# Second residual gate folded into the projection's weights, with three last weight chunks held together

## The chip, the cores and the metric

The kernel runs on one core of one Trainium2 chip. The metric is the device time of one execution in microseconds (us). The engines are named as in the profile: PE is TensorE (PEld its weight loads), DVE is VectorE, ACT is ScalarE, POOL is GpSimd, SP is SyncE, which issues nearly all DMAs.

## The reference, cut to what matters

Two model blocks follow each other on 512 tokens of width 1024, all in float32. The change is in the second layer of the first block, latent attention, and in what comes directly behind it:

```python
# mla_mixer: 16 heads of 128 values
o = jnp.einsum('bshr,rhd->bshd', o_lat, w_uv).reshape(B, S, MLA_WIDTH)   # 512 x 2048
return (o * jax.nn.silu(z)) @ w_out                                       # w_out is 2048 x 1024

# first_block, layer l = 1
x = layer_norm(DEEPNORM_ALPHA * x + (1.0 + gate[:, None, :]) * y, ln_g[l], ln_b[l])

# second_block begins
bcx = rmsnorm(h, a_pre_norm[l]) @ w_in        # b_gate, c_gate, u = split(bcx)
```

The gate is one row of 1024 values, the same for all tokens, so multiplying column n of y by 1 + gate[n] equals multiplying column n of w_out by it.

## The kernel before, in words

**Products in three parts.** A float32 product is made of three matmuls in a 32-bit fast format (`mm3`, lines 1818 to 1822): each operand is split in a high part (the value rounded) and a low part (the rest). A left operand tile is 128x128, a right one 128x512.

**The weight ring.** All weights pass through a ring of two slots, in chunks of 128x2048 values (1 MB). For each chunk SP loads `w_raw` (two DMAs, line 421) as soon as the semaphore `raw_free` of the slot says that the old chunk is split. ACT writes the high part `w_high` (`split_high`, line 743) when the load has landed (`w_full`) and PE has finished the slot's old chunk (`used`). POOL writes the low part `w_low` in eight slices of 128x256 (`low`, line 639), then frees `w_raw`. PE waits for `w_split`. At a few places DVE does the low part in one instruction (`split_low`, line 1183). Each engine's program is written out in a fixed order and only semaphores tie them together.

**The last pass of attention.** The loop over pairs of heads ends with pass `attend(7)`. It makes eight softmax units u = 0 to 7: PE scores, DVE takes the maximum (`top`), ACT exponentiates (`weigh`), DVE divides (`norm`), PE turns the result (line 2199), ACT copies it back, PE weighs values (line 2168). Between them PE does pieces of the gate projection z. In this pass ACT makes `w_high` of the projection's first chunk at u = 3.

**The projection `oout`.** Its weights are eight chunks, c = 0 to 7; chunk c holds the rows of heads 2c and 2c+1 and lies in slot c % 2. The left operand is `o_high`/`o_low`: for heads 2 to 15, ACT (line 959) and DVE (line 1529, `low_o`) make them one head at a time at the start of the projection. PE sums into eight PSUM banks, two for each tile of 128 tokens. A part, one chunk on one token tile, is 12 matmuls, and a chunk on all four tiles is 48. `out_stage` does chunks 0 to 5 on all tiles. It holds the last two chunks, 6 and 7, together: both on tile 0 and tile 1 first (tile 0's sum is then complete), and then on tiles 2 and 3:

```python
for t in range(2): part(0, t)                       # chunk 6
for t in range(2): part(1, t).then_inc(y_ready, 1)  # chunk 7: tiles 0 and 1 are complete
part(0, 2); part(0, 3); part(1, 2); part(1, 3)      # each with its increment
turn(0); turn(1)                                    # only in "oout"
```

**The boundary behind it.** For each token tile DVE multiplies the sum by the gate into `hf` (`ln_gated`, line 1426) and adds it to the scaled x (`ln_stats`, line 1431). ACT squares and takes the root (`ln_root`), DVE normalises (`ln_affine`, lines 1448 and 1449), ACT squares again (`square_x`), DVE writes `x_hat` (`prenorm`, line 1461), PE turns it (line 1949), ACT and DVE make `h_high` and `h_low` (`high_tile` line 896, `low_tile` line 1453). PE then does the first weights of the next projection, `cu`, on token tiles 0 and 1 (its two chunks, 96 matmuls of 256 columns), turns tile 2 after the first of them and tile 3 after the second, and waits for tile 3's `h_low` before it does the same two chunks on tiles 2 and 3 (the second halves). DVE makes half of the low part of `cu`'s second chunk (`split_half`, line 1389), POOL the other half (line 677).

## Time and profile before

| | before |
|---|---|
| median of three runs | 1877.47 us (1877.35 to 1878.3) |
| the profiled execution | 1876.41 us, of which the span is 1874.3 us |
| PE busy | 1807.3 us, 96% of the span |
| PEld, DVE, ACT, POOL busy | 80%, 42%, 40%, 42% |
| attention's last pass, then the projection | PE at 635.7 to 663.3 us, then to 751.4 us |
| boundary | the second halves of `cu` begin at 777.1 us |

Spans are told from the first instruction. The idle time of an engine stands in brackets behind the instruction that ended it, with what released it. Idle time of an engine that is not the bottleneck costs nothing.

### The profile page before, as it was taken

The page shows a single profiled execution, that of the slowest core. Times are in us where ns is not written, and L with a number is a line of the kernel's source. Part 1 is how long each engine was busy: PE and PEld are TensorE (multiplying, and loading weights), DVE is VectorE, ACT ScalarE, POOL GpSimd, SP SyncE. Part 2 cuts the span into 40 slices and gives each one's busy share as a digit, 9 for nine tenths or more (in the row PEclk, how much of TensorE's full clock was granted, in tenths as well). Part 3 has the DMA queues.
Part 4 walks back from the last instruction along what each step waited for, and adds up shares of the span by engine and source line. Part 5 has one row for each costly group of instructions (what it writes and reads, how often), then busy time and mean ns, then how long its engine had stood idle before and what let it go on. Part 6 is the DMA issues. An engine that isn't in the chain of part 4 may idle for free.

```text
span 1874.3 us, 24002 instructions
## 1 busy us (share of the span) xinstructions
PE 1807.3 (96%) x8798; PEld 1494.8 (80%) x8798; DVE 791.5 (42%) x1388; ACT 746.1 (40%) x1043; POOL 788.9 (42%) x992
## 2 busy tenths in 40 slices
PE   6999999989999999899999999999997999999998
PEld 6788878878788878788888888888965788888886
DVE  5775775367677632623241111103678341111102
ACT  3423331365656542322253344214456453443212
POOL 0375454354101162355335555443443135555351
PEclk9999999999999999999999999999999999999999
DMA  9543565221212132233233343232311133433321
GB/s 314 172 135 90 151 202 183 93 82 37 73 36 73 45 124 90 68 93 132 90 91 90 93 109 112 102 112 82 114 45 45 46 91 90 109 92 90 120 94 67
DMA packets 209320, 190.94 MB, mean 102 GB/s; under 512 B 10475, under 2 KB 189538, under 8 KB 209250
## 3 DMA queue, kind: packets, MB, share of 16 engines
q1 hardware_dynamic: 208608, 189.69, 32.7%
q8 instruction: 46, 0.75, 0.2%
q10 hardware_dynamic: 642, 0.29, 0.1%
q14 instruction: 24, 0.20, 0.0%
HBM read 187.86 MB, written 2.10 MB: 101 GB/s over the span
## 4 chain that ended last, share of the span: by engine, by line
PE 86%; DVE 5%; ACT 3%; POOL 3%; issue 2%; DMA 0%; SPq 0%; ACTq 0%; POOLq 0%; DVEq 0%
PE PS L1820 27%; PE PS L1822 26%; PE PS L1821 26%; POOL w_low L639 2%; PE PS L2168 1%; ACT w_high L743 1%; PE PS L1949 1%; PE PS L2199 1%; POOL w_low L677 1%; DMA ada_raw<-in_ada_w 0%; DVE soft L1775 0%; DVE probs L1773 0%; PE PS L2359 0%; PE PS L2191 0%; PE PS L2190 0%
## 5 line engine op out<-in xcount | busy, mean ns | idle before, releaser
L639 POOL TENSOR_TENSOR w_low<-w_raw,w_high 128x256 fp32r<-128x256 f32 x905 | 701.6, 811 | 841.2 <-ACT w_high L743 841.2
L1820 PE MATMUL PS<-h_high,w_high 128*128 128x512 f32 (+1 forms) x1488 | 560.7, 377 | 15.4 <-DVE h_low L1453 7.0
L1821 PE MATMUL PS<-h_low,w_high 128*128 128x512 f32 (+1 forms) x1488 | 553.7, 372 | 0.0
L1822 PE MATMUL PS<-h_high,w_low 128*128 128x512 f32 (+1 forms) x1488 | 553.6, 372 | 0.0
L743 ACT ACTIVATE w_high<-w_raw 128x2048 fp32r<-128x2048 f32 (+2 forms) x150 | 280.2, 1868 | 683.8 <-PE PS L1822 669.1
L1820 PEld LDWEIGHTS PS<-h_high,w_high 128*128 128x128 f32 x1488 | 281.6, 189 | 68.6 <-DVE h_low L1453 8.3
L1822 PEld LDWEIGHTS PS<-h_high,w_low 128*128 128x128 f32 x1488 | 281.5, 189 | 48.8
L1821 PEld LDWEIGHTS PS<-h_low,w_high 128*128 128x128 f32 x1488 | 281.8, 189 | 45.7 <-issue 0.7
L1363 DVE TENSOR_TENSOR gate_buf<-gate_buf,PS 128x512 f32<-128x512 f32 x44 | 30.3, 688 | 334.9 <-ACT gate_buf L876 334.3
L1183 DVE TENSOR_TENSOR w_low<-w_raw,w_high 128x2048 fp32r<-128x2048 f32 (+1 forms) x15 | 33.3, 2220 | 325.4 <-ACT w_high L743 325.4
L1820 PE MATMUL PS<-w_high,ff_high 128*128 128x512 f32 x352 | 137.2, 390 | 0.1
L1822 PE MATMUL PS<-w_high,ff_low 128*128 128x512 f32 x352 | 137.0, 389 | 0.0
L1821 PE MATMUL PS<-w_low,ff_high 128*128 128x512 f32 x352 | 137.0, 389 | 0.0
L667 POOL TENSOR_TENSOR w_low<-w_raw,w_high 128x256 fp32r<-128x256 f32 x35 | 29.8, 882 | 165.0 <-ACT w_high L743 165.0
L1820 PEld LDWEIGHTS PS<-w_high,ff_high 128*128 128x128 f32 x352 | 66.1, 188 | 14.6 <-POOL w_low L639 1.0
L1821 PEld LDWEIGHTS PS<-w_low,ff_high 128*128 128x128 f32 x352 | 66.1, 188 | 13.7
L1822 PEld LDWEIGHTS PS<-w_high,ff_low 128*128 128x128 f32 x352 | 66.1, 188 | 13.6
L1820 PE MATMUL PS<-w_high,o_high 128*128 128x512 f32 x192 | 75.5, 393 | 0.6 <-POOL w_low L639 0.6
L1821 PE MATMUL PS<-w_low,o_high 128*128 128x512 f32 x192 | 74.8, 389 | 0.0
L1822 PE MATMUL PS<-w_high,o_low 128*128 128x512 f32 x192 | 74.8, 389 | 0.0
L977 ACT ACTIVATE probs<-PS,soft 128x128 f32<-128x128 f32 (+1 forms) x64 | 33.8, 528 | 75.8 <-DVE soft L1573 75.8
L1367 DVE TENSOR_TENSOR ff_low<-gate_buf,ff_high 128x512 f32 x44 | 41.9, 953 | 40.8 <-ACT ff_high L880 40.8
(310 smaller groups left out, 2574.8 us busy)
## 6 DMA issues: line engine op xcount, KB each, us to landing
w_raw<-in_f_gate_up SPq DMA_DIRECT2D x88, 512.0 KB, 4.9
w_raw<-in_f_down SPq DMA_DIRECT2D x40, 512.0 KB, 4.3
w_raw<-in_e_w_in SPq DMA_DIRECT2D x32, 512.0 KB, 5.0
gains<-in_ada_w SPq DMA_DIRECT2D x16, 1024.0 KB, 5.2
w_raw<-in_a_w_in SPq DMA_DIRECT2D x24, 512.0 KB, 4.5
w_raw<-in_o_w_in SPq DMA_DIRECT2D x20, 512.0 KB, 4.3
ada_raw<-in_ada_w SPq DMA_DIRECT2D x8, 1024.0 KB, 13.3
w_raw<-in_e_w_out SPq DMA_DIRECT2D x16, 512.0 KB, 5.6
```

The source lines that it names most:

```text
L639: ins = nc.gpsimd.tensor_tensor(WL[s][:, piece], raw[s][:, piece], WH[s][:, piece].bitcast(F32), ALU.subtract)
L667: ins = nc.gpsimd.tensor_tensor(WL[1][:, piece], raw[1][:, piece], WH[1][:, piece].bitcast(F32), ALU.subtract)
L677: nc.gpsimd.tensor_tensor(WL[1][:, h:], raw[1][:, h:], WH[1][:, h:].bitcast(F32), ALU.subtract).then_inc(pool_half, 1)
L743: nact(WH[s][:, 0:n], raw[s][:, 0:n], ACT.Copy).then_inc(w_high[s], 1)
L977: nact(pm[u % 2][:, 0:w], PS[:, 2 + u % 2, 0:w], ACT.Exp, scale=MLA_SCALE, bias=soft[:, u % 2, 1, 0:1], accum_out=soft[:, u % 2, 2, 0:1]). ...
L1183: v.tensor_tensor(WL[s][:, 0:size], raw[s][:, 0:size], WH[s][:, 0:size].bitcast(F32), ALU.subtract).then_inc(w_split[s], 1)
L1363: v.tensor_tensor(buf[s][:, :], buf[s][:, :], PS[:, 2 * s + 1, :], ALU.mult).then_inc(prod_ready, 1)
L1367: v.tensor_tensor(lows[:, f, :], buf[s][:, :], fH[:, f, :].bitcast(F32), ALU.subtract).then_inc(gate_low, 1)
L1820: mm(dst, lh, rh, start=first, stop=False, skip_group_check=True)
L1821: mm(dst, lh, rl, start=False, stop=False, skip_group_check=True)
L1822: return mm(dst, ll, rh, start=False, stop=last, skip_group_check=True)
L1949: ins = tr(two(2 * t if b is None else b)[:, k, :], src[:, k * P:(k + 1) * P], ident)
```

## The change

- DVE multiplies the raw weights of each projection chunk by the gate row, in place (`gate_weights`), a 128x2048 instruction for each of the eight chunks; ACT makes `w_high` only then (new semaphores `w_gated`). The first two stand in the last pass of attention, between `top` and `norm` of u = 3 and of u = 6. The third and fourth stand between the `low_o` of heads 5 and 6 and of heads 9 and 10. The last four stand behind all heads.
- At the boundary `ln_gated` and `ln_stats` become one instruction reading PSUM (`ln_join`).
- Chunks 5, 6 and 7 are held together. Chunk 5's high and low parts go to two new tiles (`spareH`, `spareL`). PE does all three on tiles 0 and 1 first, then the five remaining parts but one, the turns of tiles 0 and 1, and the last part (chunk 7 on tile 3) behind these turns.
- ACT makes `w_high` of chunk 0 at u = 4 instead of u = 3, and of chunk 7 before chunk 6. DVE now makes the low part of chunk 6 as well as of chunk 7.
- `cu` leaves the list of projections whose second chunk is shared: POOL makes all of its low part, in eight slices, and DVE's half goes.

```diff
-        SHARED = ["cu", "gu0", "kv", "gu1"]
+        SHARED = ["gu0", "kv", "gu1"]
...
                 if name == "oout":
-                    first = 1
-                    low(0, 0)
-                    low(0, 1)
+                    for c in range(5):
+                        low(c // 2, c % 2)
+                    pool.wait_ge(w_high[1], B.split[1] + 3)
+                    for c in range(0, CHUNK, SLICE):
+                        piece = slice(c, c + SLICE)
+                        ins = nc.gpsimd.tensor_tensor(spareL[:, piece], raw[1][:, piece], spareH[:, piece].bitcast(F32), ALU.subtract)
+                    ins.then_inc(w_split[1], 1)
+                    pool.wait_ge(w_split[1], B.split[1] + 3)
+                    pool.sem_inc(raw_free[1], 1)
+                    continue
...
-                act.wait_ge(w_full[s], B.full[s] + (i + 1) * (16 * B.dmas[s]))
+                if name == "oout" and i < B.pairs:
+                    act.wait_ge(w_gated[s], i + 1)
+                else:
+                    act.wait_ge(w_full[s], B.full[s] + (i + 1) * (16 * B.dmas[s]))
...
-            highs_of("oout")
+            for c in (2, 3, 4):
+                split_high("oout", c // 2, c % 2)
+            act.wait_ge(w_gated[1], 3)
+            nact(spareH[:, :], raw[1][:, :], ACT.Copy).then_inc(w_high[1], 1)
+            act.wait_ge(w_gated[1], 4)
+            act.wait_ge(used[1], B.use[1] + 2)
+            nact(WH[1][:, :], raw[1][:, :], ACT.Copy).then_inc(w_high[1], 1)
+            split_high("oout", 3, 0)
...
+            def gate_weights(c):
+                s, B = c % 2, BASE["oout"]
+                dve.wait_ge(w_full[s], B.full[s] + (c // 2 + 1) * (16 * B.dmas[s]))
+                dve.wait_ge(gate_ready, 2)
+                w = raw[s][:, :].rearrange("p (k n) -> p k n", n=D)
+                v.tensor_tensor(w, w, gate_bc[1].unsqueeze(1).broadcast_to((P, 2, D)), ALU.mult).then_inc(w_gated[s], 1)
...
+                    if u in (3, 6) and not more:
+                        gate_weights(u // 6)
...
             for h in range(2, HEADS):
                 low_o(h)
+                if h in (5, 9):
+                    gate_weights(2 + h // 9)
+            for c in (4, 5, 7):
+                if c == 7:
+                    gate_weights(6)
+                gate_weights(c)
             split_last("oout")
+            split_low("oout", 3, 0)
             n, q = T, TR["oout"]
-            ln_gated(1, "oout", 0)
-            ln_stats(0)
-            ln_gated(1, "oout", 1)
-            ln_stats(1)
+            ln_join(0)
+            ln_join(1)
             ln_affine(n + 1, 0)
             ln_affine(n + 2, 1)
             prenorm(n + 3, 0, 3, q, x_hat1)
-            ln_gated(1, "oout", 2)
             prenorm(n + 4, 1, 3, q, x_hat1)
             low_tile(q, 0, 0)
-            ln_stats(2)
+            ln_join(2)
             low_tile(q, 1, 2)
-            ln_gated(1, "oout", 3)
-            split_half("cu")
             ln_affine(n + 5, 2)
-            ln_stats(3)
+            ln_join(3)
...
+            for c in range(5):
+                heads_ready(c)
+                for t in (2, 1, 0, 3):
+                    if c == 0:
+                        attended(t)
+                    ins = head_part(c, t)
+                ins.then_inc(used[c % 2], 1)
+            for c in (5, 6, 7):
+                heads_ready(c)
+                for t in range(2):
+                    ins = head_part(c, t)
+                    if c == 7:
+                        ins.then_inc(y_ready, 1)
+            head_part(6, 2)
+            head_part(6, 3).then_inc(used[0], 1)
+            head_part(5, 2)
+            head_part(7, 2).then_inc(y_ready, 1)
+            head_part(5, 3).then_inc(used[1], 1)
+            turn(0)
+            turn(1)
+            head_part(7, 3).then_inc(used[1], 1)
```

## Rows read from the trace of the kernel before

**Rows 1.** The profile's page: the chain that ended last, by engine.
```profile
PE 86%; DVE 5%; ACT 3%; POOL 3%; issue 2%; DMA 0%; SPq 0%; ACTq 0%; POOLq 0%; DVEq 0%
```

**Rows 2.** PE in order of time: start, duration, then operation; last pass, projection's start.
```profile
659.70 0.63 PE L2199 MATMUL PS<-small,probs 128*128 128x128 f32 x4 [0.62 <-DVE probs L1579]
...
663.26 0.47 PE L1820 MATMUL PS<-w_high,o_high 128*128 128x512 f32 x1
...
674.02 0.39 PE L1822 MATMUL PS<-w_high,o_low 128*128 128x512 f32 x1
675.03 0.50 PE L1820 MATMUL PS<-w_high,o_high 128*128 128x512 f32 x1 [0.62 <-POOL w_low L639]
```

**Rows 3.** Busy time by stretch (PE, PEld, DVE, ACT, POOL, granted clock, DMA share, GB/s).
```profile
675.00:751.00 76.00, 75.97 (x335) 62.90 (x336) 20.20 (x25) 20.66 (x21) 30.90 (x42) 1.00 0.31 97
```

**Rows 4.** PE in order of time at the boundary.
```profile
751.38 1.04 PE L1949 MATMUL PS<-small,x_hat 128*128 128x128 f32 x8
753.34 1.09 PE L1949 MATMUL PS<-small,x_hat 128*128 128x128 f32 x8 [0.92 <-DVE x_hat L1461]
757.71 0.38 PE L1820 MATMUL PS<-h_high,w_high 128*128 128x256 f32 x1 [3.28 <-DVE h_low L1453]
...
767.05 1.09 PE L1949 MATMUL PS<-small,x_hat 128*128 128x128 f32 x8 [1.86 <-DVE x_hat L1461]
...
773.73 1.03 PE L1949 MATMUL PS<-small,x_hat 128*128 128x128 f32 x8
777.14 0.39 PE L1820 MATMUL PS<-h_high,w_high 128*128 128x256 f32 x1 [2.37 <-DVE h_low L1453]
```

**Rows 5.** Busy time by stretch, columns as in rows 3: behind PE's idle time.
```profile
757.00:763.00 6.00, 5.29 (x31) 5.29 (x32) 5.89 (x6) 1.71 (x4) 2.98 (x2) 0.72 0.67 182
```

**Rows 6.** DVE instructions by line: shortest, median and longest in ns, first and last start.
```profile
L1183 DVE TENSOR_TENSOR w_low<-w_raw,w_high x15: 2018/2292/2293, 16.0 to 1847.2; 128x2048 fp32r<-128x2048 f32 x11, 128x1792 fp32r<-128x1792 f32 x4
L1529 DVE TENSOR_TENSOR o_low<-o_gated,o_high x16: 678/1213/1227, 661.5 to 679.0; 128x512 fp32r<-128x512 f32 x16
```

**Rows 7.** DVE in order of time in attention's last pass.
```profile
648.41 0.15 DVE L1573 TENSOR_SCALAR soft<-soft 128x1 f32<-128x1 f32 x1
649.41 0.16 DVE L1578 RECIPROCAL soft<-soft 128x1 f32<-128x1 f32 x1 [0.85 <-ACT probs L977]
649.61 0.49 DVE L1579 TENSOR_SCALAR probs<-probs,soft 128x512 f32<-128x512 f32 x1
...
656.63 0.11 DVE L1571 MEMSET PS<- 64x64 f32 x1
...
658.70 0.86 DVE L1579 TENSOR_SCALAR probs<-probs,soft 128x512 f32<-128x512 f32 x1
```

**Rows 8.** SP, then ACT, in order of time: the third chunk's load.
```profile
665.69 0.33 SPq L549 DMA_DIRECT2D gains<-in_ln_g  x1
...
675.28 1.92 ACT L743 ACTIVATE w_high<-w_raw 128x2048 fp32r<-128x2048 f32 x1 [1.84 <-DMA w_raw<-in_o_w_out]
```

**Rows 9.** POOL in order of time: the second, third and fourth chunk's low parts.
```profile
666.22 8.76 POOL L639 TENSOR_TENSOR w_low<-w_raw,w_high 128x256 fp32r<-128x256 f32 x8 [5.40 <-ACT w_high L743]
677.28 7.02 POOL L639 TENSOR_TENSOR w_low<-w_raw,w_high 128x256 fp32r<-128x256 f32 x8 [2.30 <-ACT w_high L743]
...
699.22 5.59 POOL L639 TENSOR_TENSOR w_low<-w_raw,w_high 128x256 fp32r<-128x256 f32 x8 [5.29 <-ACT w_high L743]
```

**Rows 10.** The shared halves by line, DVE then POOL: shortest, median, longest ns.
```profile
L1389 DVE TENSOR_TENSOR w_low<-w_raw,w_high x4: 1224/1226/2432, 758.8 to 1506.2; 128x1024 fp32r<-128x1024 f32 x4
L677 POOL TENSOR_TENSOR w_low<-w_raw,w_high x4: 2386/3444/3447, 757.8 to 1506.2; 128x1024 fp32r<-128x1024 f32 x4
```

**Rows 11.** A later load's issue on SP, then two stretches (columns as in rows 3).
```profile
684.53 0.86 SPq L421 DMA_DIRECT2D w_raw<-in_o_w_out  x2
...
688.50:689.50 1.00, 1.00 (x7) 0.81 (x6) 0.00 (x0) 0.00 (x0) 1.00 (x2) 1.00 0.43 176
689.50:691.50 2.00, 2.00 (x10) 1.68 (x9) 0.00 (x0) 0.00 (x0) 2.00 (x4) 1.00 0.00 0
```

**Rows 12.** DVE and ACT in order of time at the boundary.
```profile
751.58 1.70 DVE L1461 SCALAR_TENSOR_TENSOR x_hat<-x,stat,gains 128x1024 f32<-128x1024 f32 x1
...
755.38 1.90 ACT L743 ACTIVATE w_high<-w_raw 128x2048 fp32r<-128x2048 f32 x1
...
765.39 1.13 ACT L908 ACTIVATE h_high<-x,mv 128x1024 fp32r<-128x1024 f32 x1
...
771.96 1.28 DVE L1461 SCALAR_TENSOR_TENSOR x_hat<-x,stat,gains 128x1024 f32<-128x1024 f32 x1
```

More of the change, by code:

```diff
@@ L298, in program @@
         oL = dz("o_low", 8192, [P, HEADS, S], F32R)
+        spareH, spareL = dz("w_high_spare", 16384, [P, CHUNK], F32R), dz("w_low_spare", 18432, [P, CHUNK], F32R)
         soft = dz("soft", 22400, [P, 2, 8, 4])
@@ L372, in program @@
             sem(n) for n in ("s_done", "m_ready", "e_ready", "p_ready", "t_done", "pT_ready", "pv_done", "sz_ready", "oz_ready"))
+        w_gated = [sem(f"w_gated{s}") for s in range(2)]
         z_dve, z_pool = sem("z_dve"), sem("z_pool")
@@ L994, in attend @@
                         nact(vh[:, :, :], PS[:, 6:8, :].rearrange("p a (b n) -> p (a b) n", b=2), ACT.Copy).then_inc(kv_ready, 1)
-                    if u == 3:
-                        split_high(*(("mla", i + 1) if more else ("oout", 0)), 0)
+                    if u == 3 and more:
+                        split_high("mla", i + 1, 0)
+                    if u == 4 and not more:
+                        split_high("oout", 0, 0)
                 act.wait_ge(used[1], B.use[1] + i + 1)
@@ L1016, in _ @@
                 high_o(h)
-            highs_of("oout")
+            B = BASE["oout"]
+            for c in (2, 3, 4):
[6 more added lines that the diff above has]
+            split_high("oout", 3, 0)
             load_sqrt()
@@ L1432, in ln_stats, with ln_join @@
                 v.tensor_scalar(mv[:, t, 0:1], mv[:, t, 1:2], 1.0 / D, None, ALU.mult).then_inc(ln_stat, 1)
+            def ln_join(t):
+                wait_y(dve, 1, "oout", t)
+                if t == 0:
+                    dve.wait_ge(x_ready, T)
+                xt = x[:, t, :]
+                steps.link(v.scalar_tensor_tensor(xt, xt, ALPHA, flat2(2 * t), ALU.mult, ALU.add, accum_out=mv[:, t, 1:2]))
+                v.tensor_scalar(mv[:, t, 0:1], mv[:, t, 1:2], 1.0 / D, None, ALU.mult).then_inc(ln_stat, 1)
             def ln_factor(n, t):
@@ L2248, in _, with heads_ready, head_part @@
             turn = turner("oout", 0, x_hat1)
-            out_stage("oout", oH, oL, lambda kt: pe.wait_ge(ol_ready, kt + 1), attended, turn=turn, order=(2, 1, 0, 3))
+            B = BASE["oout"]
+            def heads_ready(c):
+                pe.wait_ge(w_split[c % 2], B.split[c % 2] + c // 2 + 1)
+                pe.wait_ge(ol_ready, 2 * c + 2)
+            def head_part(c, t):
+                wh, wl = (spareH, spareL) if c == 5 else (WH[c % 2], WL[c % 2])
+                for d in range(2):
+                    for n in range(2):
+                        w = slice(d * D + n * S, d * D + (n + 1) * S)
+                        k, rows_ = 2 * c + d, slice(t * P, (t + 1) * P)
+                        ins = mm3(PS[:, 2 * t + n, :], oH[:, k, rows_], oL[:, k, rows_], wh[:, w], wl[:, w], k == 0, k == HEADS - 1)
+                return ins
+            for c in range(5):
[19 more added lines that the diff above has]
+            head_part(7, 3).then_inc(used[1], 1)
             in_stage("cu", (TR["oout"], turn))
```

## The prediction

> **What bounds the kernel now.** I read the chain that ended last first: 86% of it is PE, so time is lost or won only where PE stands idle or slow, and I look for such places around the change [rows 1]. In order of time, PE waits 0.62 us for softmax in the last pass of attention, and 0.62 us for a low part at the projection's second chunk [rows 2]. A chunk's 48 matmuls begin 0.229 us apart, or 10.9 us in all, from the first at 663.26 to the last at 674.02 [rows 2]. From there to 751 us PE is busy for 75.97 of 76.00 us [rows 3]: the projection is bound by its matmuls, and any weight chunk that comes late costs its whole delay. At the boundary PE waits four times, 0.92 + 3.28 + 1.86 + 2.37 = 8.43 us [rows 4], and behind the 3.28 us the granted clock falls: its mean is 0.72 over 6 us, so 0.28 x 6 = 1.7 us of full clock are missing [rows 5]. In that stretch PE then waits 1.86 us all the same, so these 1.7 us are hidden.
>
> **The boundary, which is the gain.** I count from the start of chunk 5, T0. Before, three chunks (12 parts of 12 matmuls, 2.72 us each) take 32.6 us up to 751.4 [rows 4], so T0 = 718.7 and the second halves of cu, at 777.14 [rows 4], stand at T0 + 58.4. After: tile 0 is complete at T0 + 13.6 and tile 1 at T0 + 16.3; five parts follow, and the turn of tile 0 is due at T0 + 29.9. The fused join saves a pass of DVE on each tile, and x_hat of tile 1 is ready at about T0 + 27.5, so the turns don't wait. The last part ends at 29.9 + 2 x 0.95 + 2.7 = T0 + 34.5. The join of tile 2 stands between the two low_tile on DVE, so h_low of tile 1 comes about 1.6 us later and the 3.28 shrink to 1.6. Tile 2 decides next. Its root stands behind cu's second w_high on ACT, which waits for the last part: 1.9 us [rows 12]. From the root's start to the end of x_hat one tile takes 765.39 to 773.24, 7.9 us [rows 12]. POOL now makes eight slices of cu meanwhile; a DVE instruction of this chain took 1.70 instead of 1.28 us beside such slices [rows 12], 0.4 each on two of them, 0.8. So tile 2 turns at T0 + 34.5 + 0.1 + 1.9 + 7.9 + 0.8 = T0 + 45.2. From there PE's own work and the last wait are as before: 773.73 - 767.05 = 6.7 and 777.14 - 773.73 = 3.4 us [rows 4]. Sum T0 + 55.3: a gain of 3.1 us. Its bounds: 1.5 us if the slices hold every two-input instruction, 4.5 us if neither they nor ACT's order cost anything.
>
> **The multiplies in softmax.** A multiply isn't in the trace. The nearest row is DVE's 128x2048 instruction with two inputs from SBUF, 2.29 us [rows 6]. The first begins at 648.56, when top(3) ends; norm(3) began at 649.41 and ended at 650.10 [rows 7]. It now ends at 648.56 + 2.29 + 0.7 = 651.55, 1.45 us later, and PE's turn of u = 3 and all behind it move with it. Of the second multiply about 1.1 us lie in DVE's wait for ACT. Top(7), at 656.63 before [rows 7], starts behind it at about 659.25: 2.6 us later, which nothing takes up (the 0.62 us of idle are of this chain). Moving chunk 0's w_high to u = 4 costs nothing, as it lies in ACT's wait before u = 7. So the projection begins 2.65 us later, at 665.9. Chunk 1's low part is then in time, because DVE stops after four heads to wait and POOL runs alone: the 0.62 us and some 0.2 us around it go. Chunk 1 starts **1.9 us late**, at 676.9, and PE wants chunk 2 at 687.9. Bounds of this term: 0 if the fillers take up the delay, 2.7 if chunk 1 still waits.
>
> **Chunk 2, the largest term.** SP sends the gains and then this chunk only behind the last gated head, from 665.69, and ACT got it at 675.28, having waited for the DMA [rows 8]: 9.6 us. Moved by 2.65 it lands at 677.9. Before, ACT made w_high at once and POOL ran from 677.28 to 684.3 [rows 9], 1.6 us ahead of PE. Now DVE multiplies first, to 680.2 (all behind it in DVE's queue, the heads 6 to 15, waits too), ACT takes 1.9 us and POOL begins at 682.2. Alone it needs 5.6 us [rows 9], which would be 687.8, just in time. It isn't alone: DVE has ten heads and the multiply of chunk 3 before it. That the two take turns, one instruction each, is in the rows: the eight slices beside low_o took 8.76 us [rows 9], so 1.15 us for each pair, and low_o took 1213 ns instead of 678 [rows 6]. And a long instruction holds the other for all its length: POOL's half takes 2386 ns alone and 3444 when DVE's of 1224 goes first; DVE's takes 2432 when POOL's goes first [rows 10]. So: 0.9 us to the end of the first slice, 2.15 for the multiply of chunk 3, 0.6 for a slice, and six pairs of 1.15 with the last six heads: 682.2 + 0.9 + 2.15 + 0.6 + 6.9 = 692.7. PE waits **4.8 us**. Bounds: 0 (POOL alone) and 6.5 (two slices more beside DVE, a landing 0.5 us later).
>
> The Trainium skill, "SBUF — State Buffer", section "SBUF: two separate sides", says that a DVE instruction with two SBUF inputs and a GpSimd instruction that reads SBUF hold a shared port pair by turns, each for the whole instruction, and don't share its bandwidth. [Rows 10] agree. By it the wait is the 4.8 us; read as a mere slowing of each POOL slice to 1.15 us, it would be 3.1.
>
> **The clock.** PE's idle 3.28 us at the boundary were followed by missing clock worth 1.7 us [rows 5]; I expect the same behind 4.8 us in the midst of full work: **+1.5 us**.
>
> **The last chunks.** A load takes 5.2 us from POOL's last slice to its end: POOL ends at 684.30, SP issues at 684.53, and the transfers are over at 689.5 [rows 9, 11]. From chunk 2's low part at 692.7: chunk 3 split at 698.3; chunk 5 landed 703.7, multiplied 706.0, its POOL part behind chunk 4's (712.8 with the slower clock) to 718.4; chunk 7 landed 723.8, multiplied 726.1, ACT makes chunk 7 and then chunk 6 to 730.0, DVE both low parts to 732.7. PE has done chunk 5 on tiles 0 and 1 at 732.3 and waits **0.5 us**. The wait falls on chunk 6, though it is chunk 7 that is late, as chunk 6 stands behind it on ACT. Bounds 0 and 3.
>
> **The sum.** 1.9 + 4.8 + 1.5 + 0.5 = 8.7 us lost, 3.1 won: 5.6 us slower. It passes to the end whole, as PE is the chain behind it. The profiled execution's 1876.4 (span 1874.3) become 1882.0; the runs' median lies 1.1 us above it: 1877.5 + 5.6 = **1883.1**.
>
> **The rivals.** (a) Chunk 2 is in time, because DVE and POOL hold each other less than I count. The wait and the clock's drop go, the tail costs 0.8: 1.9 + 0.8 - 3.1, so 1877.1, no difference. It decides whether chunk 2's low part ends before 687.9. Against it stand rows 10. (b) Faster: a multiply costs PE nothing, neither in softmax nor by holding POOL. The place is DVE's queue: its waits there, 0.85 us at a time [rows 7], would have to swallow a multiply, which is so only if it lasts under 0.9 us, against the 2.29 us of rows 6. Then there is no loss, the boundary gives 3.1 and its 0.8 us of slices: 1877.5 - 3.9 = 1873.6. For it speaks only that the trace holds no multiply of this form. (c) Slower still: the loads of chunks 5 and 7, in one chain now, come later than 5.2 us behind their release, towards the 9.6 us of the third chunk's [rows 8]; at 7.9 each it is 2 x 2.7 = 5.4 us more, 1888.5. Against it: no gains travel with them.
>
> **How the numbers follow.** The forecast has 0.62 (its own range 1880 to 1887), (a) 0.18, (b) 0.10, (c) 0.10. What a measurement of this kernel can tell from no change is 0.2%, 3.75 us. Faster by more: (b), 0.10. Within: (a) and 0.06 of the forecast, where the bounds of the boundary and chunk 2 meet, 0.24. Slower: 0.66. For 8 in 10 the range takes in (a) and leaves (b) and most of (c) out: 1876 to 1887.5.
>
> **What would show it.** In the profile after: norm of u = 3 ends about 1.5 us after it did, the projection begins near 665.9; PE's longest wait, near 5 us, stands at the third chunk and names POOL's w_low; POOL's slices there include one near 2.8 us; the granted clock falls behind it; PE waits under 3 us at chunk 6; the two turns don't wait; the waits at the boundary are near 1.6, 3 and 2.4 us. I am wrong if PE runs through chunk 2, or if the second halves come earlier than 777.1.

## The result and the profile after

The changed kernel takes 1882.34 us (median of 7 runs, 1880.90 to 1886.66), the kernel before 1876.77 us beside it (7 runs, 1875.12 to 1878.30). The ratio is 1.0032, with an interval of 1.0023 to 1.0042: it is slower, by 5.6 us between the medians and by 6.0 us by the ratio. The prediction was 5.6 us slower.

The profiled execution of the changed kernel took 1886.66 us, span 1884.9: the longest of its seven. Its steps are read one by one below; its sum is not the median's. 1.3 us of its excess arise before the change: POOL begins its last run of attention's weights at 630.69 in the trace of before and at 631.98 here. I count each trace from that run, R, and write an instant as R + so much.

The chain that ended last, by engine, of the kernel after:

```profile
PE 85%; DVE 5%; POOL 3%; ACT 3%; issue 1%; DMA 1%; SPq 0%; POOLq 0%; ACTq 0%; DVEq 0%
```

It is as in [rows 1]: PE still sets the end, so its waits are the account. PE's waits from 635 to 800 us of the kernel after, by what ended them: us in total, times, longest us.

```profile
PE PS L1862 <- POOL w_low L641: 3.8, 1, 3.8
PE PS L1862 <- DVE h_low L1484: 3.6, 2, 2.4
PE PS L1991 <- DVE x_hat L1492: 2.9, 1, 2.9
PE PS L2241 <- DVE probs L1617: 2.8, 2, 1.5
PE PS L2210 <- ACT probs_t L995: 0.8, 1, 0.8
PE PS L1862 <- DVE w_low L1205: 0.7, 1, 0.7
```

And PE in order of time, kernel after:

```profile
652.82 0.63 PE L2241 MATMUL PS<-small,probs 128*128 128x128 f32 x4 [1.23 <-DVE probs L1617]
...
663.21 0.63 PE L2241 MATMUL PS<-small,probs 128*128 128x128 f32 x4 [1.55 <-DVE probs L1617]
664.61 3.86 PE L2210 MATMUL PS<-probs_t,v_heads 128*128 128x512 f32 x8 [0.78 <-ACT probs_t L995]
...
668.23 0.48 PE L1862 MATMUL PS<-w_high,o_high 128*128 128x512 f32 x1
...
694.05 0.50 PE L1862 MATMUL PS<-w_high,o_high 128*128 128x512 f32 x1 [3.78 <-POOL w_low L641]
...
728.46 0.39 PE L1862 MATMUL PS<-w_high_spare,o_high 128*128 128x512 f32 x1
...
734.73 0.50 PE L1862 MATMUL PS<-w_high,o_high 128*128 128x512 f32 x1 [0.67 <-DVE w_low L1205]
...
765.23 0.39 PE L1862 MATMUL PS<-h_high,w_high 128*128 128x256 f32 x1 [1.22 <-DVE h_low L1484]
774.10 1.97 PE L1991 MATMUL PS<-small,x_hat 128*128 128x128 f32 x8 [2.86 <-DVE x_hat L1492]
...
786.93 0.51 PE L1862 MATMUL PS<-h_high,w_high 128*128 128x256 f32 x1 [2.37 <-DVE h_low L1484]
```

The projection begins at 668.23, R + 36.2, where [rows 2] have 663.26, R + 32.6: 3.7 us later. The 0.62 us at its second chunk [rows 2] are gone. The third chunk begins at 694.05 behind a wait of 3.78 us, the longest here; in [rows 3] there was none at all in this stretch. Chunk 6 costs 0.67 us. At the boundary one of the four waits of [rows 4] is gone, the 0.92 before tile 1's turn, and the 3.28 has become 1.22; but the wait for tile 2's x_hat has grown from 1.86 to 2.86, and the last is 2.37 as before. Chunk 5 begins at 728.46, R + 96.5, where T0 was 718.7, R + 88.0: 8.5 us later. The second halves of cu begin at R + 155.0, against R + 146.5 in [rows 4]: 8.5 us later too.

Part of this is the clock. Busy time by stretch (columns as in rows 3), kernel after:

```profile
664.00:668.00 4.00, 3.39 (x6) 1.82 (x7) 1.95 (x3) 3.97 (x6) 1.69 (x3) 0.57 0.00 0
694.00:700.00 6.00, 5.95 (x19) 4.73 (x20) 0.61 (x1) 0.00 (x0) 5.56 (x8) 0.72 0.52 175
773.00:780.00 7.00, 5.90 (x28) 5.90 (x29) 5.33 (x7) 3.28 (x7) 1.63 (x1) 0.53 0.54 150
786.00:792.00 6.00, 5.07 (x30) 5.07 (x30) 0.88 (x1) 0.00 (x0) 0.00 (x0) 0.72 0.01 3
```

The granted clock falls four times to its lower level: behind the short waits in softmax (0.43 x 4 = 1.7 us of full clock missing), behind the third chunk (0.28 x 6 = 1.7), behind the 2.86 us at the boundary (0.47 x 7 = 3.3), and once more behind the 2.37 us, where the second halves have begun (0.28 x 6 = 1.7, on top of the 8.5 us above). Before, it fell once here, for 1.7 us that lay under a wait [rows 5]. DVE and POOL in the projection, kernel after:

```profile
649.78 2.29 DVE L1567 TENSOR_TENSOR w_raw<-w_raw,gains 128x2048 f32<-128x2048 f32 x1
651.99 0.16 DVE L1616 RECIPROCAL soft<-soft 128x1 f32<-128x1 f32 x1
...
679.14 2.29 DVE L1567 TENSOR_TENSOR w_raw<-w_raw,gains 128x2048 f32<-128x2048 f32 x1 [4.68 <-DMA w_raw<-in_o_w_out]
681.35 2.49 DVE L1560 TENSOR_TENSOR o_low<-o_gated,o_high 128x512 fp32r<-128x512 f32 x4
683.75 2.83 DVE L1567 TENSOR_TENSOR w_raw<-w_raw,gains 128x2048 f32<-128x2048 f32 x1
686.51 6.91 DVE L1560 TENSOR_TENSOR o_low<-o_gated,o_high 128x512 fp32r<-128x512 f32 x6
...
704.89 2.29 DVE L1567 TENSOR_TENSOR w_raw<-w_raw,gains 128x2048 f32<-128x2048 f32 x1 [3.01 <-DMA w_raw<-in_o_w_out]
```

```profile
683.46 10.54 POOL L641 TENSOR_TENSOR w_low<-w_raw,w_high 128x256 fp32r<-128x256 f32 x8 [6.32 <-ACT w_high L755]
694.17 5.56 POOL L641 TENSOR_TENSOR w_low<-w_raw,w_high 128x256 fp32r<-128x256 f32 x8 [0.18 <-POOL w_low L641]
```

The same POOL slices from 683 to 695 us, shortest, median and longest in ns:

```profile
L641 POOL TENSOR_TENSOR w_low<-w_raw,w_high x10: 727/1170/2784, 683.5 to 694.9; 128x256 fp32r<-128x256 f32 x10
```

The multiply takes 2.29 us, the bound taken from [rows 6]. Chunk 2 is multiplied at 679.14, when its load has landed; ACT and POOL follow, and POOL needs 10.54 us for eight slices, where 5.56 us do when DVE is silent (the next row). Of the eight one took 2.78 us: it stood behind the multiply of chunk 3, which itself took 2.83. The median of 1.17 us is the pair that [rows 9] gave as 1.15. It is less than the two instructions take alone, 0.68 and 0.70 us (5.56 us for eight slices), which add up to 1.38: each holds the other for most of its length, not for all of it.

### The profile page after: what moved, and what is told of

It is laid out like the page before. It is cut to its first block, busy times and chain, and to the rows that moved or that the text cites. A ratio compares the mean times of both kernels' runs of the same rounds, so it can differ in the third digit from the quotient of the medians.

```text
span 1884.9 us, 24002 instructions
## 1 busy us (share of the span) xinstructions
PE 1814.2 (96%) x8798; PEld 1499.8 (80%) x8798; DVE 805.5 (43%) x1392; ACT 745.9 (40%) x1043; POOL 790.4 (42%) x991
## 4 chain that ended last, share of the span: by engine, by line
PE 85%; DVE 5%; POOL 3%; ACT 3%; issue 1%; DMA 1%; SPq 0%; POOLq 0%; ACTq 0%; DVEq 0%
PE PS L1862 26%; PE PS L1863 26%; PE PS L1864 26%; POOL w_low L641 2%; PE PS L2210 1%; ACT w_high L755 1%; PE PS L1991 1%; PE PS L2241 1%; DMA w_raw<-in_o_w_out 1%; POOL w_low L679 1%; DMA ada_raw<-in_ada_w 1%; DVE soft L1817 0%; DVE probs L1815 0%; DVE w_raw L1567 0%; PE PS L2233 0%
## 5 line engine op out<-in xcount | busy, mean ns | idle before, releaser
L755 ACT ACTIVATE w_high<-w_raw 128x2048 fp32r<-128x2048 f32 (+2 forms) x148 | 276.4, 1868 | 666.1 <-PE PS L1864 646.0
L1862 PE MATMUL PS<-w_high,o_high 128*128 128x512 f32 x176 | 70.1, 398 | 4.5 <-POOL w_low L641 3.8
L1863 PE MATMUL PS<-w_low,o_high 128*128 128x512 f32 x176 | 69.3, 394 | 0.0
L1864 PE MATMUL PS<-w_high,o_low 128*128 128x512 f32 x176 | 69.1, 393 | 0.0
```

Of the source, the lines that this page charges most:

```text
L755: nact(WH[s][:, 0:n], raw[s][:, 0:n], ACT.Copy).then_inc(w_high[s], 1)
L1862: mm(dst, lh, rh, start=first, stop=False, skip_group_check=True)
L1863: mm(dst, lh, rl, start=False, stop=False, skip_group_check=True)
L1864: return mm(dst, ll, rh, start=False, stop=last, skip_group_check=True)
```

## The experiments

All twelve beside the kernel before, the ratio to its runs on the same chip. The edits shown are against the kernel after, cut to their main lines, unless another is named. "No multiply" and "join only" leave the gate out and "two multiplies" applies it twice to two chunks, so these three don't compute the reference and only measure time. "Second halves" is their start counted from R in the profiled run (before: +146.5); "waits" are PE's of 0.3 us and more there, from 645 us on: softmax / projection / boundary.

| kernel | ratio (interval) | median, us | waits in the profiled run, us | second halves |
|---|---|---|---|---|
| after | 1.0032 (1.0023 to 1.0042) | 1882.34 | 1.23, 1.55, 0.78 / 3.78, 0.67 / 1.22, 2.86, 2.37 | +155.0 |
| fold, two held | 1.0043 (1.0030 to 1.0057) | 1885.43 | 1.23, 1.55, 0.78 / 4.44 / 3.96, 2.37 | +153.0 |
| hold only | 0.9995 (0.9986 to 1.0004) | 1876.35 | 0.78 / 1.01 / 1.23, 3.14, 2.37 | +144.9 |
| no multiply | 0.9980 (0.9970 to 0.9990) | 1872.64 | 0.78 / 1.01 / 1.22, 2.85, 2.37 | +142.7 |
| load first | 1.0048 (1.0034 to 1.0061) | 1885.15 | as after / 0.61, 2.67 / as after | +152.8 |
| heads first | 1.0052 (1.0039 to 1.0065) | 1886.87 | as after / 3.43, 2.64 / as after | +156.9 |
| POOL gates | 1.0035 (1.0022 to 1.0048) | 1883.87 | 0.78 / 1.01, 4.96, 0.42 / as after | +154.9 |
| all three | 1.0027 (1.0017 to 1.0038) | 1882.76 | 0.78 / 1.01, 0.89, 0.31, 2.49 / as after | +150.2 |
| DVE spare | 1.0006 (0.9998 to 1.0015) | 1878.50 | 0.78 / 1.02, 0.93, 0.33, 0.96, 1.38 / as after | +150.2 |
| tail order | 1.0009 (1.0000 to 1.0019) | 1878.93 | 0.6, 0.78 / 2.32 / as after | +148.8 |
| two multiplies | 1.0014 (1.0005 to 1.0023) | 1880.19 | 1.22, 1.52, 0.78 / none / 0.94, 3.28, 1.12, 2.37 | +149.4 |
| join only | 0.9999 (0.9990 to 1.0008) | 1878.22 | 0.78 / 1.01 / 3.96, 2.37 | +144.8 |
| hold, early high | 0.9991 (0.9982 to 1.0000) | 1876.53 | 0.6, 0.78 / 0.63 / 1.20, 3.15, 2.37 | +145.0 |

**Taking the change apart.** The first three separate its halves. "Fold, two held": the multiplies and the join as in the change, chunks 6 and 7 alone held together.

```diff
-            for c in (5, 6, 7):
-                heads_ready(c)
...
+            out_stage("oout", oH, oL, lambda kt: pe.wait_ge(ol_ready, kt + 1), attended, turn=turn, order=(2, 1, 0, 3))
```

> The change without its second half: the weights are multiplied and the boundary has the fused join, but only chunks 6 and 7 are held together, as before. Theory (the loss comes from the multiplies: softmax 1.9 us, chunk 2 late by 4 to 5 us, a drop of the clock behind it 1.5 us): PE still waits 4 to 5 us for POOL's low part at the third chunk, and as the turns of tiles 0 and 1 have no part behind them the boundary gives back only 1 to 2 us: 5 to 8 us slower than the kernel before, 1882 to 1885. Rival (holding three chunks and the late last chunks are what costs): within 2 us of the kernel before.

"Hold only": three chunks held, none multiplied, and the boundary with its gated passes on DVE.

```diff
-                if h in (5, 9):
-                    gate_weights(2 + h // 9)
...
-            ln_join(0)
-            ln_join(1)
+            ln_gated(1, "oout", 0)
+            ln_stats(0)
+            ln_gated(1, "oout", 1)
+            ln_stats(1)
```

> The other half alone: three chunks are held, chunk 5 in its own tiles, cu's second chunk is POOL's alone, but no weight is multiplied; the gate is applied at the boundary as before (ln_gated, then ln_stats). Theory: no wait at the third chunk nor in softmax; the boundary keeps 1 to 3 us: 1 to 3 us faster than the kernel before, 1874 to 1876. Rival: 3 us or more slower, since the last three chunks or POOL's eight slices of cu cost more than the covered turns give.

"No multiply": the changed kernel without its eight multiplies (and so without the gate); ACT waits for the loads instead.

```diff
-                if name == "oout" and i < B.pairs:
-                    act.wait_ge(w_gated[s], i + 1)
-                else:
-                    act.wait_ge(w_full[s], B.full[s] + (i + 1) * (16 * B.dmas[s]))
+                act.wait_ge(w_full[s], B.full[s] + (i + 1) * (16 * B.dmas[s]))
```

> The changed kernel with its eight multiplies left out (so the gate is not applied to y at all) and ACT waiting for the loads instead. Everything else stands. Theory: it prices the multiplies with all they cause at 7 to 10 us, so this kernel is 2 to 5 us faster than the kernel before, 1872 to 1875. Rival: it stays slower than the kernel before by more than 2 us.

The loss is the multiplies': with them 1.0032, without them 0.9980, so they cost 0.52%, 9.8 us, with the clock's falls that came with them (the prediction's terms of loss add up to 8.7). What they bought is the boundary, 0.20% or 3.7 us without them (predicted 3.1). In its profiled run the second halves begin 3.8 us earlier than before, and its three waits at the boundary are those of the kernel after. PE in order of time, and a stretch behind its wait (columns as in rows 3), of "no multiply":

```profile
754.12 0.39 PE L1851 MATMUL PS<-h_high,w_high 128*128 128x256 f32 x1 [1.22 <-DVE h_low L1481]
762.98 1.09 PE L1980 MATMUL PS<-small,x_hat 128*128 128x128 f32 x8 [2.85 <-DVE x_hat L1489]
773.07 0.38 PE L1851 MATMUL PS<-h_high,w_high 128*128 128x256 f32 x1 [2.37 <-DVE h_low L1481]
```

```profile
763.00:772.00 9.00, 7.70 (x64) 7.46 (x64) 5.64 (x7) 3.38 (x5) 0.51 (x1) 1.00 0.43 118
```

The waits are those of the kernel after to 0.01 us, yet here the clock stays at 1.00, and there its mean was 0.53 over 7 us. So the boundary's waits were in both what the change makes them; whether the clock's fall comes on top differs between them.

"Fold, two held" came out as expected (5 to 8 us slower; 8.1 by the ratio) and is the slowest of the three, but its interval and that of the kernel after overlap (1.0030 to 1.0057, 1.0023 to 1.0042): beside the multiplies, holding the third chunk is worth some 2 us, not certainly, and in the two profiled runs the second halves come earlier without it (R + 153.0, R + 155.0), as the clock's fall at the boundary was half as long there. "Hold only" missed its forecast of 1 to 3 us: it is not told apart from before, and by its interval the held chunk alone wins at most 0.14%.

**The third chunk.** "Load first": SP sends the loads of chunks 2 and 3 before it waits for the last gated head and sends the gains.

```diff
+            for s in range(2):
+                load("oout", 1, s, deep(s, w_in["o_w_out"], 4 + s * 2))
             sp.wait_ge(oz_ready, HEADS + CREDIT)
...
-            with sp.Fori(1, 4) as i:
+            with sp.Fori(2, 4) as i:
```

> The changed kernel, with SP sending the loads of the third and fourth chunk ahead of its wait for the last gated head and of the three gains. Theory: the third chunk lands about 6 us earlier, DVE multiplies it right behind head 5, POOL starts near 679 instead of 682 to 683 and ends its ten contended microseconds near 689 to 690, so PE's wait there falls from 3.8 to 1 to 2 us and the clock no longer drops behind it: 3 to 5 us faster than the changed kernel. Rival (the wait is POOL's turns with DVE alone, whenever it starts): within 1 us of the changed kernel.

The wait at the third chunk goes, as it should, 0.61 us come back at the second, and the kernel gets no faster, where 3 to 5 us were expected (1.0048 beside 1.0032 of another session, intervals overlapping). PE, then POOL, in order of time, "load first":

```profile
678.92 0.50 PE L1864 MATMUL PS<-w_high,o_high 128*128 128x512 f32 x1 [0.61 <-POOL w_low L643]
...
730.89 0.50 PE L1864 MATMUL PS<-w_high,o_high 128*128 128x512 f32 x1 [2.67 <-DVE w_low L1207]
```

```profile
668.52 10.35 POOL L643 TENSOR_TENSOR w_low<-w_raw,w_high 128x256 fp32r<-128x256 f32 x8 [4.02 <-ACT w_high L757]
680.41 8.59 POOL L643 TENSOR_TENSOR w_low<-w_raw,w_high 128x256 fp32r<-128x256 f32 x8 [1.54 <-ACT w_high L757]
692.23 7.64 POOL L643 TENSOR_TENSOR w_low<-w_raw,w_high 128x256 fp32r<-128x256 f32 x8 [3.23 <-ACT w_high L757]
```

The multiply now lies beside chunk 1's slices, which take 10.35 us instead of 7.42, and the next runs of POOL are met by one as well (7.64 instead of 5.56). The weights' chain is late all the same, only further on: the wait at chunk 6 is 2.67 instead of 0.67, and the clock's fall stands behind that one. Here chunk 2 is in time, as in the prediction's rival (a), though by an earlier load and not by a shorter run of POOL, and it did not give the 1877.1 us that (a) was priced at. (a)'s "tail costs 0.8" leaves out what these runs show: when PE does not wait at chunk 2, it comes to chunk 6 earlier by those microseconds, and the chain behind does not.

"Heads first": chunk 3's multiply behind all the heads' low parts.

```diff
-                if h in (5, 9):
-                    gate_weights(2 + h // 9)
+                if h == 5:
+                    gate_weights(2)
+            gate_weights(3)
```

> The changed kernel with one line moved: DVE multiplies chunk 3 behind the low parts of all heads, not between heads 9 and 10. Theory (a long DVE instruction holds POOL for its whole length, and chunk 2's low part is what PE waits for): the slice of nearly 2.8 us goes from POOL's run on chunk 2, which takes 8.3 instead of 10.5 us; PE's wait at the third chunk falls from 3.8 to 1.5 to 2 us, and the wait at chunk 6 grows by about the same up to 2.7 us, as that chain starts from the same place: within 2 us of the changed kernel in the whole, on the faster side. Rival (POOL's run is long for another reason): the run stays above 10 us.

This missed, and its rival came: the run stays above 10 us. DVE and POOL in order of time, "heads first":

```profile
680.76 9.37 DVE L1560 TENSOR_TENSOR o_low<-o_gated,o_high 128x512 fp32r<-128x512 f32 x10
690.05 2.81 DVE L1567 TENSOR_TENSOR w_raw<-w_raw,gains 128x2048 f32<-128x2048 f32 x1
```

```profile
682.88 10.56 POOL L641 TENSOR_TENSOR w_low<-w_raw,w_high 128x256 fp32r<-128x256 f32 x8 [6.04 <-ACT w_high L755]
```

When POOL begins, some of the ten heads are done, and fewer are left than POOL has slices; the multiply, moved behind them, meets POOL's last slice instead of its second. The run takes 10.56 us, 10.54 before the edit. Where in the queue a long instruction stands does not matter to that run so long as it falls within it. It does to the next: chunk 3's low part now takes 7.63 us from 694.88, not 5.56 from 694.17, and PE waits 2.64 us at chunk 6 instead of 0.67. The ratio, 1.0052, is higher than 1.0032, but the two intervals touch.

**The multiplies in softmax.** "POOL gates": the first two multiplies on POOL, in sixteen slices, ahead of its low parts.

```diff
-                    if u in (3, 6) and not more:
-                        gate_weights(u // 6)
...
+                            ins = nc.gpsimd.tensor_tensor(raw[s][:, piece], raw[s][:, piece], gate_bc[1][:, c % D:c % D + SLICE], ALU.mult)
```

> The changed kernel with the first two multiplies done by POOL, in eight slices each, while it has nothing else to do in the last pass of attention; DVE's softmax is left as before the change. Theory: the two waits of PE in softmax (1.2 and 1.6 us) go, the drop of the clock at the projection's start goes with them, and the projection begins 3 to 3.6 us earlier against the pass; the third chunk's load and all behind it move with it: 3 to 4 us faster than the changed kernel, about 1878 to 1880. Rival (that time is taken up later by the waits for weights): under 1 us.

The two waits in softmax go and the projection starts 1.4 us earlier (R + 34.8), with 1.01 us of waiting at its first chunk in place of none. PE, then a stretch behind (columns as in rows 3), "POOL gates":

```profile
692.41 0.80 PE L1867 MATMUL PS<-w_high,o_high 128*128 128x512 f32 x1 [4.96 <-POOL w_low L641]
```

```profile
688.00:698.00 10.00, 5.58 (x15) 4.47 (x16) 4.31 (x5) 1.46 (x1) 9.82 (x12) 0.66 0.30 105
```

All that was won is waited for at the third chunk (4.96 us instead of 3.78), and the clock's drop about it is twice as long (0.34 x 10 = 3.4 us missing, part of it while PE waits; from the third chunk to the fourth it is 13.1 us instead of 10.9): 1.0035, as after. The rival, that the gain is taken up later, was right.

"Two multiplies" asks the reverse, what softmax alone pays: the kernel before (the edit is against it) with only the two multiplies in softmax and chunk 0's `w_high` at u = 4, so that chunks 0 and 1 are gated twice.

```diff
+                    if u in (3, 6) and not more:
+                        gate_weights(u // 6)
                     if u in PIECES and more:
```

> The kernel before, with nothing added but the change's two multiplies in the last pass of attention and ACT's high part of chunk 0 at u = 4. The boundary is as before, so the weights of chunks 0 and 1 carry the gate twice. Theory (the two multiplies hold softmax, PE waits 1.2 and 1.6 us there, and the clock drops once at the projection's start, which costs as much again as one of them): the projection begins 3.5 us later against the pass, and 2.5 to 4 us show in the whole. Rival (only the 2.2 us of waits count, and the drop of the clock comes from the rest of the change): 1.5 to 2.2 us.

Ratio 1.0014: 2.6 us, of the kernel's 6.0. The projection starts at R + 36.4, and in the kernel after at R + 36.2, so all 3.7 us of that term belong to these two instructions with what they bring on, and the third chunk is then in time. The stretch before the projection (columns as in rows 3), "two multiplies":

```profile
664.00:668.00 4.00, 3.58 (x6) 1.95 (x7) 2.15 (x3) 3.97 (x6) 1.50 (x3) 0.57 0.00 0
```

The same drop to 0.57 as after. It is present in every profiled run where both softmax multiplies are DVE's (five kernels) and absent in the nine others, before among them.

**The tail.** "All three": load first, heads first and POOL gates together.

```diff
+            for s in range(2):
+                load("oout", 1, s, deep(s, w_in["o_w_out"], 4 + s * 2))
...
+            gate_weights(3)
...
+                            ins = nc.gpsimd.tensor_tensor(raw[s][:, piece], raw[s][:, piece], gate_bc[1][:, c % D:c % D + SLICE], ALU.mult)
```

> The changed kernel with three moves together: the first two multiplies on POOL, chunk 3's multiply behind all heads, the third and fourth chunk's loads ahead of the wait for the last head and the gains. Theory: no wait in softmax and none above 0.7 us at the third chunk; what stays is the chain to the last chunks (POOL's low part of chunk 5, the load of chunk 7, its multiply, ACT's two high parts, DVE's two low parts), 2.5 to 3 us at chunk 6, with a drop of the clock behind it: 3 to 5 us faster than the changed kernel, 1877 to 1880. Rival (the multiplies can be hidden wholly by order): as fast as the kernel without multiplies, 1873.

"DVE spare": the same, with chunk 5's low part one DVE instruction instead of eight POOL slices.

```diff
+                if c == 5:
+                    dve.wait_ge(w_high[1], BASE["oout"].split[1] + 3)
+                    v.tensor_tensor(spareL[:, :], raw[1][:, :], spareH[:, :].bitcast(F32), ALU.subtract).then_inc(w_split[1], 1)
```

> As the kernel with three moves, and DVE, which is idle there, makes the low part of chunk 5 in one instruction as soon as ACT has its high part, instead of POOL behind chunk 4's. Theory: the load of chunk 7 goes out 5 to 9 us earlier, the chain to the last chunks is in time, PE doesn't wait at chunk 6, and the clock doesn't drop: 2 to 4 us faster than with three moves, 1873 to 1876, so faster than both kernels. Rival (the chain ends at ACT and DVE, which make chunks 7 and 6 one after the other): the wait stays above 1.5 us.

With every earlier wait near 1 us or under it, 2.49 us stay at chunk 6 (1.0027, where 1877 to 1880 us were expected and 1882.76 measured). With chunk 5's low part on DVE it is 1.38 and the ratio 1.0006: better, but not the kernel "faster than both" that was expected. DVE in order of time, "DVE spare":

```profile
709.44 2.86 DVE L1677 TENSOR_TENSOR w_low_spare<-w_raw,w_high_spare 128x2048 fp32r<-128x2048 f32 x1 [1.99 <-ACT w_high_spare L1037]
718.36 2.29 DVE L1569 TENSOR_TENSOR w_raw<-w_raw,gains 128x2048 f32<-128x2048 f32 x1 [6.07 <-DMA w_raw<-in_o_w_out]
721.87 2.29 DVE L1569 TENSOR_TENSOR w_raw<-w_raw,gains 128x2048 f32<-128x2048 f32 x1 [1.21 <-DMA w_raw<-in_o_w_out]
```

The buffer of chunk 7 is free at 712.3, and its load lands 9.6 us later, where 5.2 is usual: SP issues it behind chunk 6's, whose buffer POOL frees only at 712.9, and the two land 3.5 us apart. "Tail order" turns the two round, in SP's list and in DVE's, and makes the first two high parts earlier (the edit is against "DVE spare").

```diff
-            with sp.Fori(2, 4) as i:
-                for s in range(2):
-                    load("oout", i, s, deep(s, w_in["o_w_out"], i * 4 + s * 2))
+            for i, s in ((2, 0), (2, 1), (3, 1), (3, 0)):
+                load("oout", i, s, deep(s, w_in["o_w_out"], i * 4 + s * 2))
...
+                    split_high("oout", 0, 1)
...
+            for c in (4, 5, 7, 6):
```

> The kernel in which DVE makes chunk 5's low part, with three orders changed: SP sends the load of chunk 7 ahead of chunk 6's and DVE multiplies it first (in the kernel with chunk 5's low part on DVE, SP's queue held chunk 7's load behind chunk 6's); ACT makes chunk 0's high part at u = 3 again, which POOL's multiplies allow, and chunk 1's ahead of the last Silu. Theory: PE's 1.4 us at chunk 6 and the three waits of about 1 us for POOL at the first chunks go: 2 to 4 us faster than that kernel, 1874.5 to 1876.5, at or just below the kernel before. Rival (what is left of the loss lies in the clock's drops at the boundary): within 1 us of it.

DVE, then PE, in order of time, "tail order":

```profile
706.14 2.52 DVE L1672 TENSOR_TENSOR w_low_spare<-w_raw,w_high_spare 128x2048 fp32r<-128x2048 f32 x1 [3.34 <-ACT w_high_spare L1034]
713.99 2.29 DVE L1566 TENSOR_TENSOR w_raw<-w_raw,gains 128x2048 f32<-128x2048 f32 x1 [5.32 <-DMA w_raw<-in_o_w_out]
```

```profile
689.51 0.68 PE L1863 MATMUL PS<-w_high,o_high 128*128 128x512 f32 x1 [2.32 <-POOL w_low L642]
```

Chunk 7 now lands 5.3 us after its buffer is free, and the waits at chunks 0, 1, 4 and 6 are gone. But the third chunk waits again, 2.32 us, and behind it the clock falls (columns as in rows 3):

```profile
689.00:695.00 6.00, 5.49 (x17) 4.41 (x18) 0.32 (x1) 0.19 (x1) 5.82 (x9) 0.72 0.55 175
```

It takes 1.0009, not told apart from "DVE spare"; the 2 to 4 us expected did not come. All these edits have won back some 0.25% of the 0.52% that the multiplies cost, across sessions; the kernel is back near the time of before, with the boundary's gain spent on them.

**The gains by themselves.** "Join only": no multiplies (and no gate), two chunks held, the fused join at the boundary.

```diff
-                if h in (5, 9):
-                    gate_weights(2 + h // 9)
...
-            for c in (5, 6, 7):
-                heads_ready(c)
...
+            out_stage("oout", oH, oL, lambda kt: pe.wait_ge(ol_ready, kt + 1), attended, turn=turn, order=(2, 1, 0, 3))
```

> No multiplies (the gate is not applied to y at all), two chunks held as before, the fused join at the boundary and cu's second chunk left to POOL alone: the fourth corner beside the changed kernel, the one with two chunks held, and the one without multiplies. Theory: the join alone gives 1 to 2 us (1875 to 1876), and holding the third chunk gives 2 to 3 us on top of it, as without the multiplies nothing at the end is late. Rival (holding the third chunk is worth nothing by itself): as fast as the kernel with three held and no multiplies, 1872.6.

Ratio 0.9999, where 1 to 2 us were expected, and 0.9980 with the third chunk held as well. Neither half gives anything that the timed runs can tell by itself: the join leaves PE a wait of 3.96 us at the boundary, for want of matmuls, and the held chunk gives PE matmuls but leaves 3.14 us at tile 2, which still has DVE's gated pass before it. In their profiled runs both begin the second halves some 1.6 us earlier than before, and both let PE wait 1.01 us at chunk 0, whose high part is made later in them. From the start of chunk 5 to the second halves it is 58.4 us before, 57.0 in "hold only", 56.9 in "join only" and 54.7 in "no multiply": 1.4 and 1.5 us won singly, 3.7 together. The clock differs in these stretches (1.7 us of full clock missing in "hold only", 3.3 in "join only", none in "no multiply"), and each single interval leaves room for about 2 us. So it is not shown that the halves together give more than their sum. The join needs the multiplies in any case.

"Hold, early high" is "hold only" with chunk 0's high part back at u = 3, what can be kept of the change without multiplies.

```diff
-                    if u == 3 and more:
-                        split_high("mla", i + 1, 0)
-                    if u == 4 and not more:
-                        split_high("oout", 0, 0)
+                    if u == 3:
+                        split_high(*(("mla", i + 1) if more else ("oout", 0)), 0)
```

> Three chunks held and no multiply, with the gate applied at the boundary as before, and ACT's high part of chunk 0 back at u = 3, where the kernel before has it. Theory (that move, made for the multiplies, left PE waiting 1.0 us for POOL at chunk 0 in both kernels without multiplies): the wait goes and the kernel is 1 us faster than the one with three chunks held: 1 to 2.5 us faster than the kernel before, the one version that has the gain of holding and keeps the result. Rival (the 1.0 us is taken up at the boundary): as that kernel, 0 to 1 us.

PE's waits from 630 to 800 us, "hold, early high", columns as above:

```profile
PE PS L1982 <- DVE x_hat L1487: 3.1, 1, 3.1
PE PS L1853 <- POOL w_low L641: 0.8, 2, 0.6
```

The projection starts at R + 32.6, as before the change (R + 33.3 in "hold only"); the 1.01 us at chunk 0 are gone, and 0.63 us stand at chunk 1, like the 0.62 of [rows 2]. It took 0.9991 of the time of before, 0.9982 to 1.0000: some 1.7 us less, at the edge of what can be told, and the lowest ratio of the kernels here that compute all of the reference; "hold only" (0.9995) is not told apart from it.

## Why the prediction was right

The direction, the size (5.6 us; 5.6 between the medians) and the place of the largest loss were right. Its terms, in the profiled run:

| term | predicted | measured |
|---|---|---|
| chunk 1 later | 1.9 | 3.0 (694.05 - 1.3 - 675.03 - 10.9 - 3.78) |
| wait at the third chunk | 4.8 | 3.78 |
| clock behind it | 1.5 | 1.7 |
| last chunks | 0.5 | 0.67 |
| boundary | -3.1 | -0.7; -3.7 where the clock does not fall |

The loss adds up to 9.2 (8.7 predicted), less 0.7 is the 8.5 us of the second halves.

**Softmax** was right in its mechanism: the reciprocal behind the first multiply starts at 651.99, 1.3 us later than 649.41 when counted from R, 1.45 predicted. What failed is "the projection begins 2.65 us later": it began 3.7 later. The delays alone came out smaller than counted: counted from R, PE's last turn of the pass is 2.2 us late (663.21 against 659.70). The rest is the drop at 664, which I had not counted: the eight matmuls behind that turn take 3.86 us, and before

```profile
661.11 2.39 PE L2168 MATMUL PS<-probs_t,v_heads 128*128 128x512 f32 x8 [0.78 <-ACT probs_t L983]
```

which is 1.5 us more. "Two multiplies" has the same drop with nothing else of the change but `w_high` at u = 4. The wait at chunk 1 went, as predicted. "Moving chunk 0's w_high to u = 4 costs nothing" holds only where DVE's multiplies delay softmax: in "hold only" PE waits 1.01 us at chunk 0.

**The third chunk**: POOL's run was put at 0.9 + 2.15 + 0.6 + 6.9 = 10.55 us, and took 10.54. It started at 683.46, which is the forecast 682.2 with the trace's offset of 1.3, and ended at the forecast 692.7 on the same count. The wait came out 1.0 us smaller because PE itself was 1.1 us later than forecast: the two misses are one. The Trainium skill ("SBUF — State Buffer", section "SBUF: two separate sides") states that of a DVE instruction with two SBUF inputs and a GpSimd instruction that reads SBUF, the one that starts first holds the shared ports for its whole length and blocks the other. The trace agrees in kind: a slice of 2.78 us beside the multiply, multiplies of 2.83 us where they meet a slice in full and 2.29 where they don't, and "heads first", where moving the multiply left the run as long. It does not agree to the last tenth: a pair takes 1.17 us, not the 1.38 of both lengths; the sum came out because it was priced with the measured pair.

**The clock** behind the wait was right at 1.7 (1.5).

**The tail** was right at 0.67, chunk 6 the place. The loads landed as counted: chunk 5 at 704.89, 5.2 us behind POOL's end at 699.73. Chunk 7's landed 5.3 us behind POOL's end as well (725.67, 720.34). So rival (c) had nothing. Rival (b) fell with the 2.29 us of the multiply. Rival (a)'s price was too low for its tail, if it went as in "load first".

**The boundary** was right without the multiplies ("no multiply": 3.7), and the forecast waits 1.6, 3 and 2.4 came as 1.22, 2.86 and 2.37. In the profiled run of the kernel after, 3.0 us of the gain go to the clock's drop at 773. Why the same waits bring no drop in one run, 3.4 us at the lower level in others ("all three", "DVE spare", "load first", "heads first", "tail order") and 6.8 in two (after, "POOL gates") stays open; no experiment controlled it. How often it happens in the runs that were only timed cannot be seen; that the kernel's median lies 4.3 us under its profiled run says that the profiled one is not typical. So the terms above are one execution's: they leave 8.5 us at the second halves, not 5.6, and the agreement of the forecast with the median is partly luck.

## What to carry to other kernels

Folding a scale into weights moves work from the end of a stage to the path that feeds it: ask first how much slack that path has, chunk by chunk up to the last, since a wait removed at one chunk came back at the next late one. Two engines that lock each other out cost nearly the sum of their instructions (1.17 us for 0.68 and 0.70 here), so an instruction added on one is to be charged to the other's run wherever they overlap. And where several waits in a row bound a boundary, measure the halves of a change together as well as singly: here neither alone could be told from no change, and the two together gave 3.7 us.

## What the runs showed of the hardware

Short waits can be followed by a fall of the clock too. Waits of 1.23 us at 652 and of 1.55 and 0.78 us from 661 were followed by a drop of 1.7 us of full clock, while 0.78 and 1.01 us in "no multiply", or 0.62, 0.78 and 0.62 before, were followed by none. I had priced the clock only behind the one long wait.

POOL's low part of a chunk took 5.56 us with DVE silent, 7.42 with four heads' low parts beside it, and 10.54 with DVE busy all the time, two inputs from SBUF in each of its instructions: nearly twice the time for the same work. DVE's join, whose second input is in PSUM, was not held. At the boundary, all within one run of POOL (766.10 to 774.64), DVE in order of time, kernel after:

```profile
767.79 1.53 DVE L1479 SCALAR_TENSOR_TENSOR x<-x,mv,gains 128x1024 f32<-128x1024 f32 x1
769.35 1.64 DVE L1480 SCALAR_TENSOR_TENSOR x<-x,stat,gains 128x1024 f32<-128x1024 f32 x1
770.92 1.21 DVE L1462 SCALAR_TENSOR_TENSOR x<-x,PS 128x1024 f32<-128x1024 f32 x1
```

The first two, with two inputs from SBUF, take 1.53 and 1.64 us instead of 1.28; the join, as large, takes 1.21, as it does with POOL silent (1.21 at 762.64). Not every one with two is held as long: the next, x_hat at 772.74, takes 1.31.
